# The last gate's modulation lane by lane on VectorE, the seams between projections cleared, and new branch and drain orders, in a one-core two-block fp32 kernel

## The reference, cut to what matters

```python
def second_block(x, c, ctx, c_ctx, w_mod, b_mod, ...):
    silu_c = jax.nn.silu(c)
    for l in range(DEPTH_2):                       # 2 layers
        mod = silu_c @ w_mod[l] + b_mod[l]         # 1x2048 @ 2048x6144
        shift, scale, gate = jnp.split(mod[:, None, :], 3, axis=-1)
        ...
        h = rmsnorm(x, norm_g[l]) * (1.0 + scale) + shift
        u = h @ w_in[l]                            # e_w_in, then o_w_in
        ...                                        # mixers a, b (l = 0); c, d (l = 1)
        x = x + gate * (y @ w_o[l])
    return rmsnorm(x, final_g)
```

## Time and profile before

| | |
|---|---|
| median of 3 runs | 2984.72 us (2983.91 to 2986.87) |
| the profiled execution | 2982.89 us, span of its trace 2981.1 us |
| PE busy | 2936.4 us, 99% |
| DVE busy | 1924.8 us, 65% |
| ACT busy | 1266.2 us, 42% |
| POOL busy | 217.6 us, 7% |
| DMA | 611.09 MB, mean 205 GB/s |

### The profile page before, as it was taken

The page is one execution under the profiler, slowest core; times in us unless marked ns, Lnnn a source line. Parts: engine busy times, 40 slices in busy tenths (PEclk is TensorE's granted clock), DMA queues, the critical chain, the costliest instruction groups (busy, mean ns, idle before and its releaser), DMA issues.

```text
span 2981.1 us, 37294 instructions
## 1 busy us (share of the span) xinstructions
PE 2936.4 (99%) x14159; PEld 2403.4 (81%) x14159; DVE 1924.8 (65%) x2700; ACT 1266.2 (42%) x2045; POOL 217.6 (7%) x308
## 2 busy tenths in 40 slices
PE   8999999999999999999999999999999999999998
PEld 7897788878888888888887877777888887877877
DVE  5886466668868888888865734454544534666655
ACT  5443354543444444443555223333333324435444
POOL 1000000011001010010100000000000100102000
PEclk9999999999999999999999999999999999999999
DMA  8987956568768878878865733333343624776444
GB/s 271 299 296 270 311 177 189 149 194 279 260 211 267 275 265 275 269 261 275 268 205 172 246 126 113 117 113 121 107 134 121 217 87 141 246 237 202 138 134 160
DMA packets 315426, 611.09 MB, mean 205 GB/s; under 512 B 29373, under 2 KB 90010, under 8 KB 314352
## 3 DMA queue, kind: packets, MB, share of 16 engines
q1 hardware_dynamic: 296012, 544.74, 56.5%
q0 software_dynamic: 18272, 62.64, 6.0%
q10 hardware_dynamic: 964, 1.33, 0.2%
HBM read 567.94 MB, written 41.85 MB: 205 GB/s over the span
## 4 chain that ended last, share of the span: by engine, by line
PE 93%; DVE 3%; ACT 1%; issue 1%; DMA 0%; SPq 0%; POOL 0%; POOLq 0%; ACTq 0%; DVEq 0%
PE acc L686 28%; PE acc L688 27%; PE acc L687 27%; PE acc L1507 3%; PE acc L1477 2%; PE acc L1495 2%; DVE w_lo L508 1%; PE acc L1067 1%; PE acc L1475 1%; PE acc L1455 1%; ACT w_hi L502 1%; PE acc L715 1%; PE acc L781 0%; DMA raw<-in_w_in 0%; PE acc L616 0%
## 5 line engine op out<-in xcount | busy, mean ns | idle before, releaser
L686 PE MATMUL acc<-w_hi,a_hi 128*128 128x512 f32 (+3 forms) x3736 | 1483.0, 397 | 10.3 <-DVE w_lo L508 6.8
L688 PE MATMUL acc<-w_hi,a_lo 128*128 128x512 f32 (+3 forms) x3736 | 1448.2, 388 | 0.0
L687 PE MATMUL acc<-w_lo,a_hi 128*128 128x512 f32 (+3 forms) x3736 | 1446.6, 387 | 0.0
L508 DVE TENSOR_TENSOR w_lo<-raw,w_hi 128x1024 fp32r<-128x1024 f32 (+3 forms) x778 | 932.6, 1212 | 384.4 <-ACT w_hi L502 378.8
L502 ACT ACTIVATE w_hi<-raw 128x1024 fp32r<-128x1024 f32 (+3 forms) x778 | 805.4, 1047 | 731.3 <-PE acc L688 671.3
L686 PEld LDWEIGHTS acc<-w_hi,a_hi 128*128 128x128 f32 x3736 | 703.5, 188 | 167.7 <-issue 21.5
L688 PEld LDWEIGHTS acc<-w_hi,a_lo 128*128 128x128 f32 x3736 | 702.6, 188 | 142.7
L687 PEld LDWEIGHTS acc<-w_lo,a_hi 128*128 128x128 f32 x3736 | 704.2, 188 | 126.6
L545 DVE SCALAR_TENSOR_TENSOR lanes_b<-raw,ct,lanes_b 128x1024 f32<-128x1024 f32 x150 | 189.5, 1304 | 0.0
L545 DVE SCALAR_TENSOR_TENSOR lanes_c<-raw,ct,lanes_c 128x1024 f32<-128x1024 f32 x120 | 156.7, 1348 | 0.0
L1553 ACT ACTIVATE pb<-acc,at_st 128x256 f32<-128x256 f32 (+4 forms) x144 | 71.1, 494 | 139.8 <-DVE at_st L1665 91.8
(11 more groups left out here) (431 smaller groups left out, 1767.8 us busy)
## 6 DMA issues: line engine op xcount, KB each, us to landing
raw<-in_w_mod SPq DMA_DIRECT2D x192, 512.0 KB, 4.8
raw<-in_w_in SPq DMA_DIRECT2D x128, 512.0 KB, 5.0
raw<-in_w_mlp_in SPq DMA_DIRECT2D x128, 512.0 KB, 4.4
raw<-in_w_mlp_out SPq DMA_DIRECT2D x128, 512.0 KB, 5.4
raw<-in_e_w_in SPq DMA_DIRECT2D x104, 512.0 KB, 4.4
raw<-in_w_o SPq DMA_DIRECT2D x64, 512.0 KB, 5.0
raw<-in_o_w_in SPq DMA_DIRECT2D x64, 512.0 KB, 4.8
raw<-in_w_in SPq DMA_DIRECT2D x56, 448.0 KB, 4.6
```

The costliest lines, as they stand in the source:

```text
L508: nc.vector.tensor_tensor(w_lo[:, n % SPLITS, 0:size], raw[:, r % RAWS, 0:size], w_hi[:, n % SPLITS, 0:size].bitcast(F32), ALU.subtract)\
L686: nc.tensor.matmul(o, s.lhs(0, kt, tt), wh, start=kt == 0 and not s.goes_on, stop=False)
L687: nc.tensor.matmul(o, s.lhs(0, kt, tt), wl, start=False, stop=False)
L688: last = nc.tensor.matmul(o, s.lhs(1, kt, tt), wh, start=False, stop=end)
```

## The change

Half 0 of the last gate goes to DVE as half 1 does, as `gate_vec` with 32 chunks in place of 16: its 16 chunks are put one to each weight chunk of steps 1 and 2 of `out2`, the lane sum on PE behind chunk 1 of step 3, and ACT's copy and store behind chunk 3. The seam `RowStep`s, `MV`, `row_t` and their semaphores go. The turns of units 8 and 9 at the first seam move ahead of the last ahead-chunk, and the first two turns at the second seam ahead of `out2`'s last chunk. `branch` becomes the `next` of `gates_c`. In `Region.dve`, the result is written ahead of `lo`, and in a drain one iteration earlier. `hi_at` is always two places ahead.

```diff
@@ stages
-        def mod_step(n, bank):
-            return RowStep([wcols(A["w_mod_2"][1], 2 * j, 2 * DM + n * G) for j in range(8)], [(bank, 0)], None, ...)
-        for run in (("qkv0", "qkv", "qkv_end", "gates_a", "gates_b", "gates_c"),
+        for run in (("qkv0", "qkv", "qkv_end", "gates_a", "gates_b", "gates_c", "branch"),
-        gate_vec = Matvec([(A["w_mod_2"][1], 2 * DM + CH)])
+        gate_vec = Matvec([(A["w_mod_2"][1], 2 * DM + j * CH) for j in range(2)])
+        for q in range(KT):
+            stages["out2"].steps[1 + q // 8].mods.setdefault(q % 8, []).append((gate_vec, q))
...
-        seam_rows = [mod_step(0, 7), mod_step(1, 7)]
@@ the lane sums
-        stages["in3_g0"].hook("pe", 0, 3, gate_lanes)
-        stages["in3_g0"].hook("act", 0, 7, gate_keep)
+        stages["out2"].hook("pe", 3, 1, lambda pe: gate_lanes(pe, 0))
+        stages["out2"].hook("act", 3, 3, lambda act: gate_keep(act, 0))
+        stages["in3_g0"].hook("pe", 0, 3, lambda pe: gate_lanes(pe, 1))
+        stages["in3_g0"].hook("act", 0, 7, lambda act: gate_keep(act, 1))
@@ the seams
         def ahead_tiles(pe):
             for c in range(s_.ahead):
                 f5.ready(pe, c)
                 pe_chunk(pe, s_, c, 0, 4)
-            f5_turn(pe, 8)
-            f5_turn(pe, 9)
+                if c == 2:
+                    f5_turn(pe, 8)
+                    f5_turn(pe, 9)
-        stages["out2"].hook("pe", 3, 7, lambda pe: first_turns(pe))
+        stages["out2"].hook("pe_pre", 3, 7, lambda pe: first_turns(pe))
-            for c in range(8):
-                stages[a].hook("pe", end, 7, lambda pe, n=n, c=c: pe_rows(pe, seam_rows[n], c))
-            stages[b].hook("act", 0, 6, lambda act, n=n: rows_keep(act, n))
@@ Region
-                    big = where[first[x] - 1][0][0].pairs
-                    hi = max(first[x] - (1 if big else 2), free, -1)
+                    hi = max(first[x] - 2, free, -1)
@@ Region.dve
-                    for u in range(p.U + 4):
+                    for u in range(p.U + 3):
                         if 0 <= u - 1 < p.U and p.units[u - 1].pair:
                             self.join(dve, link, p, u - 1)
+                        if 4 <= u <= p.U:
+                            self.result(dve, link, p, u - 4)
+                        if 0 <= u - 1 < p.U and p.units[u - 1].pair:
                             self.lo(dve, p, u - 1)
-                        if 0 <= u - 4 < p.U:
-                            ...
...
-                        if u <= p.U + 2:
-                            self.silu(dve, p, u)
-                            if u >= p.U or not p.units[u].pair:
-                                self.lo(dve, p, u)
-                            for feed, x in p.turns.get(u, ()):
-                                feed.lo(dve, x)
+                        self.silu(dve, p, u)
+                        if u >= p.U:
+                            self.result(dve, link, p, u - 3)
+                        if u >= p.U or not p.units[u].pair:
+                            self.lo(dve, p, u)
+                        for feed, x in p.turns.get(u, ()):
+                            feed.lo(dve, x)
```

More of the change, by code:

```diff
@@ L704, in pe_rows @@
                 pe.wait_ge(landed[r % RAWS], 16 * (r // RAWS + 1))
-                if c == 0 and s in seam_rows[1:]:
-                    pe.wait_ge(row_free, seam_rows.index(s))
-                elif c == 0 and s is cmp_rows_of[0]:
+                if c == 0 and s is cmp_rows_of[0]:
                     pe.wait_ge(cmp_there, 1)
@@ L713, in pe_rows @@
                 j = 32 * (kt % 4)
-                lhs = s.lhs(kt) if s.lhs is not None else MV[:, kt:kt + 32]
-                last = nc.tensor.matmul(acc[j:j + 32, bank, 0:w], lhs, raw[:, r % RAWS, k * w:(k + 1) * w],
+                last = nc.tensor.matmul(acc[j:j + 32, bank, 0:w], s.lhs(kt), raw[:, r % RAWS, k * w:(k + 1) * w],
                                         start=kt < 4, stop=kt >= len(s.chunks) * s.wtiles - 4)
@@ L718, in pe_rows @@
                 last.then_inc(row_used, 1)
[L720 to L728, removed]
         def ahead_tiles(pe):
@@ L1582, in join, with result @@
                                                op0=ALU.mult, op1=ALU.add).then_inc(pair_done, 1)
+            def result(self, dve, link, p, i):
+                if i == 0 and p.saves0:
+                    dve.wait_ge(at_saved, 16 * p.saves0)
+                w, v = p.units[i], p.u0 + i
+                st = at_st[:, v % 8, :]
+                dve.wait_ge(o_done, v + 1)
+                if w.add:
+                    dve.wait_ge(e_done, v)
+                if w.sink is not None and p.guard:
+                    link(nc.vector.tensor_scalar(st[:, 1:2], st[:, 1:2], st[:, 2:3], TINY,
+                                                 ALU.add, ALU.max))
+                elif w.sink is not None:
+                    link(nc.vector.tensor_tensor(st[:, 1:2], st[:, 1:2], st[:, 2:3], ALU.add))
+                elif p.guard:
+                    link(nc.vector.tensor_scalar(st[:, 1:2], st[:, 1:2], TINY, None, ALU.max))
+                link(nc.vector.reciprocal(st[:, 3:4], st[:, 1:2]))
+                if w.coeff is not None and not w.pair:
+                    link(nc.vector.tensor_tensor(st[:, 3:4], st[:, 3:4], w.coeff, ALU.mult))
+                o = acc[:, self.obanks[v % len(self.obanks)], 0:P]
+                if w.add:
+                    nc.vector.scalar_tensor_tensor(out=w.out, in0=o, scalar=st[:, 3:4], in1=w.out,
+                                                   op0=ALU.mult, op1=ALU.add).then_inc(e_done, 1)
+                elif w.gate is not None:
+                    if i == 0 and p.kept:
+                        for bank, _ in p.kept.tiles:
+                            dve.wait_ge(acc_free[bank], p.kept.fill[bank] + 1)
+                    elif i == 0:
+                        dve.wait_ge(gate_there, 16 * p.gates_end)
+                    if i == 0:
+                        for feed, x in p.turned_first:
+                            feed.turned(dve, x)
+                    nc.vector.scalar_tensor_tensor(out=w.out, in0=o, scalar=st[:, 3:4], in1=w.gate,
+                                                   op0=ALU.mult, op1=ALU.mult).then_inc(e_done, 1)
+                else:
+                    nc.vector.tensor_scalar(w.out, o, st[:, 3:4], None, ALU.mult)\
+                      .then_inc(e_done, 1)
             def dve(self, dve):
@@ L1874, in two_blocks @@
         sub_row = place("sub_row", [P, HD], SCR[0] + 35904)
-        row_t = place("row_t", [P, G], SCR[0] + 33792)
         mid_t = place("mid_t", [P, 2, G], SCR[0] + 4096)
@@ L2118, in out2_rows @@
                 dve.wait_ge(rt_pow, 4 + r // 4)
+            if r == 1:
+                dve.wait_ge(gate_sum, 1)
             if r >= 2:
@@ L2966, in _ @@
                 if n == 3:
-                    sp.wait_ge(row_out, 32)
+                    sp.wait_ge(gate_out, 16)
                     wait_step(sp, "in3", 1)
```

105 lines of the change are left out of this document (28 added, 77 removed).

## The result

The changed kernel takes 2989.85 us (median of 14 runs, 2987.87 to 2994.0) against 2983.52 us (14 runs, 2982.17 to 2986.87) of the kernel before on the same chips: a ratio of 1.0022, 95% interval 1.0013 to 1.0030. It is 6.3 us slower, where I had forecast 9.1 us faster. Its profiled execution has a span of 2988.4 us.

A forecast was written before the change was run, and what follows sets the result against it. PE, busy 99% of the span, was taken to bound the kernel. Terms for seams, drains and clock summed to -9.1 us, from a median of 2984.72 to 2975.6 us; the 8-in-10 range was 2971.5 to 2981.

The forecast's parts named there:

- the other drains: Drains in D, `at3` and `at2`: +1.6, -1.2, +1.8 and -0.8 us; the rest 0, with a `w_lo` to spare.
- The clock behind the first drain of `at1`: `w_lo` behind the last result: stand of 2.0 us, +2.2, no clock fall taken; a fall would add 1.7.
- third fall: Clock also falling behind the new 2.0 us stand at the first drain of `at1`: 2980.7 us.
- rival 1: Clock still falls behind the shortened stands at the end of `at1` and in `at2`: -5.7 us, 2979.0 us; chance 0.18.
- the seams: Two places where 32 row matmuls go, 3.57 us of PE each: -7.1 us, no wait behind the moved turns.
- the lane sum: The sum for the gate's half 0, added on PE once more in `out2`: +1.0 us.
- the DVE work in `out2`: 16 lane operations of 1.30 us, 20.9 us, hidden behind the chunks' own matmuls: 0.
- the stand at 2008: Third drain of `at2`, wait for `oA`: result and `pt` come first, -1.5 us, and no slow clock behind, -1.7.
- the first two D drains: First: `w_lo` behind the last result, +1.6 us; second: result ahead of the rotary work, -1.2 us.
- The two drains estimated by analogy: First of C and third of D in `at3`, shaped like the first of D: 0.9 us each, +1.8.
- the end of `at1`: Result ahead of the `a_lo`, so `branch`'s first `w_lo` is earlier: -1.7 us, and -1.7 for the clock.
- The rival of the other side: Slower: DVE's lane operations in `out2` delay each of 16 chunks by up to 1.30 us: +11.8, 2996.5 us; chance 0.04.

The follow-up runs named there:

- Experiments 1 and 5: Changed kernel with, first, the last result back at its iteration's end: 2965.4 us; second, the next pass's rotary work ahead of the last result: 2981.71 us.
- experiment 3: Kernel before with only the gate's first half moved to DVE in `out2` and the seams cleared: 2976.48 us, 0.9978.
- experiment 8: Kernel before with only `branch` added to the first run of stages, its first chunk split inside `at1`: 2978.22 us, 0.9984.
- experiment 4: Kernel before with only `Region.dve` and `result` of the changed kernel, the new drain order: 2998.66 us, 1.0051.

## Why the prediction was wrong

- **The step that failed** is the last sentence on the other drains: "The rest have a `w_lo` to spare: 0." It was wrong for the first two drains of `at2` and for the third behind its stand, which measured +6.86, +3.61 and +3.32. What I compared was the `w_lo` of each drain with the start of its chunk, moving only the result. At the first two, and for 1.30 us of the third, I had not moved what stands between the result and the next `w_lo`: the rotary work, which before filled the wait for the last product and now comes after it. The other 2.02 us of the third are the `w_lo` directly behind the result, the very mechanism that I had priced at `at1` and left out here. The rows were there to be read, since the trace before shows these twelve operations, at the first drain, ending 0.03 us before the last product starts. For the second D drain I used the same move, as a gain ("the result now comes ahead of the rotary work"), and did not ask what it does where the rotary work was cover. Experiments 1 and 5 show it.
- **The clock behind the first drain of `at1`** was my second miss: +3.86 for +2.2. I held 1.96 us to be harmless because one such stand had been. The fall was in the prediction as the upper bound of that term and as the "third fall" of rival 1, but the sum held it at 0. Behind the stands that I shortened, which rival 1 was mainly about, the clock stayed full (1.57 and 0.80 us).
- **On the same clock**, the Trainium skill (TensorE: Matmul & The Clock Gate, "What's actually happening") says that the observation of activity is free-running, so that where a transition falls depends on its phase. These traces agree with it, though none shows the phase: the same stand, in the same kernel, had once a full and once a slow clock behind it (3.30 and 3.31 us). By the granted clocks measured here, such a stand should have had a price between 0 and 1.7 us in the sum, and not 0.
- **Right in mechanism and size**: the seams (-7.3 for -7.1), the lane sum (+1.2 for +1.0), the DVE work in `out2` hidden (experiment 3), the stand at 2008 (-3.35 for -3.2), the first two D drains (+1.44, -1.23 for +1.6, -1.2). The two drains estimated by analogy were +0.66 and +1.06 for 0.9 each.
- **Right in size, wrong in reason**: the end of `at1`. I credited the result ahead of the `a_lo`; experiment 8 shows that the branch split alone gives 4.26, and experiment 4 that the new order alone gives 0.4.
- **The rival of the other side** was placed in `out2`, with the lane operations as its mechanism. The slower outcome came from the drain order instead, for which I had named no rival but one in which it costs nothing.

By parts: gate and seams -6.5 us, branch -4.6, `w_hi` two places early -0.7 (the part that is shown), drain order +15.7 by itself. The sum is +3.9, where +6.3 was measured. Of the 2.4 us between, 1.3 are at the end of `at1`, where branch alone gives 4.26, the order alone 0.36, and both 3.35. The rest is not settled; falls of the clock in one kernel and not in another are of that size.

The version that beats both kernels is `late_last`: everything of the change, with the last unit's result behind the work that does not need it, 2965.4 us, 0.58% under the kernel before.

## What to carry to other kernels

In a queue that runs in order, moving an instruction that waits ahead of ones that don't turns its wait into idle time and puts all that it passed behind it. Count the passed work up to the next thing that the bounding engine needs, not only the neighbour: here 5.5 us of rotary work lay between at one place, and a single `w_lo` of 1.2 us was enough at others. A wait at the end of a pass is a place for filler, and the filler is worth the wait that it covers.

## What was not expected of the hardware

I read the granted clock over the 4.5 us behind every stand of PE of over 0.9 us, from 30 us on, in all 13 profiles here. It stayed full behind all stands of up to 1.78 us and fell behind all three of 5.3 us. Of 23 stands between 1.9 and 3.4 us it fell behind 14 and stayed full behind 9: full behind 1.96 us in the kernel before, slow behind 1.96 in the changed one; full behind 3.30 and slow behind 3.31 us at the same place of the same kernel. One such fall is +1.56 us by the matmuls, the only large difference between the two profiles of the changed kernel.
